# The delta rule's inverse: its transpose made on VectorE in blocks of 32 by 32, and the state's product ahead of the output's

## What is computed

```python
decay = exp(where(causal, g[:, None] - g[None, :], -inf))
m = where(strict, beta[:, None] * (k @ k.T) * decay, 0.0) + eye(C)
wu = triangular_solve(m, concatenate([k * (beta * exp(g)), v * beta]), lower=True)
w_c, u_c = wu[:, :Dh], wu[:, Dh:]
attn = (q @ k.T) * decay
def step(state, chunk):
    v_new = u_c - w_c @ state
    o = (q * exp(g)) @ state + attn @ v_new
    state = state * exp(g_last) + (k * exp(g_last - g)).T @ v_new
```

## Time and profile before

| What | Value |
|---|---|
| Time, median of 3 runs | 3366.05 us (3365.32 to 3366.66) |
| Span of the profiled execution | 3364.8 us (no time of its own is given beside it) |
| Granted TensorE clock | 0.997 of full speed |
| TensorE busy | 3322.3 us, 99% |
| VectorE busy | 2191.7 us, 65% |
| ScalarE busy | 1711.6 us, 51% |
| HBM read | 580.05 MB, 173 GB/s over the span |

### The profile page before, as it was taken

One profiled execution on the slowest core, in us unless ns is written; L12 is line 12 of the kernel. 1 busy time (PEld: TensorE's weight loads), 2 busy tenths in 40 slices (PEclk: granted clock), 3 DMA queues, 4 the chain that ended last, 5 costly groups with the idle time before them and its releaser, 6 DMA issues. The chain is left out here.

```text
span 3364.8 us, 72970 instructions
## 1 busy us (share of the span) xinstructions
PE 3322.3 (99%) x27834; PEld 3282.9 (98%) x27834; DVE 2191.7 (65%) x3584; ACT 1711.6 (51%) x2803; POOL 309.8 (9%) x314
## 2 busy tenths in 40 slices
PE   8999999999999999999999999999999999999999
PEld 7999999999999998899999999999899999999999
DVE  7667666656656666678755665665778755666655
ACT  5555644434434455656544554444665654554443
POOL 1010100000000025011002200001012101210000
PEclk9999999999999999999999999999999999999999
DMA  5234555555555554444455545555444455445554
GB/s 190 107 112 148 176 186 189 189 186 187 188 187 187 187 187 159 139 163 158 161 197 184 183 161 188 188 201 177 146 153 163 156 178 209 172 162 188 187 206 162
DMA packets 90629, 584.28 MB, mean 174 GB/s; under 512 B 10480, under 2 KB 11120, under 8 KB 28400
## 3 DMA queue, kind: packets, MB, share of 16 engines
q1 hardware_dynamic: 88992, 577.47, 48.7%
q0 software_dynamic: 1488, 4.72, 0.4%
HBM read 580.05 MB, written 2.10 MB: 173 GB/s over the span
## 5 line engine op out<-in xcount | busy, mean ns | idle before, releaser
L172 DVE TENSOR_TENSOR w_lo<-raw,w_hi 128x768 fp32r<-128x768 f32 (+5 forms) x1202 | 1378.5, 1159 | 372.6 <-ACT w_hi L161 365.6
L191 PE MATMUL bank<-h,w_hi 128*128 128x256 f32 x5168 | 1459.3, 282 | 16.5 <-DVE w_lo L172 12.0
L161 ACT ACTIVATE w_hi<-raw 128x768 fp32r<-128x768 f32 (+4 forms) x1190 | 1095.7, 968 | 692.3 <-PE bank L193 615.4
L193 PE MATMUL bank<-h,w_lo 128*128 128x256 f32 x5168 | 1444.1, 279 | 0.0
L192 PE MATMUL bank<-h,w_hi 128*128 128x256 f32 x5168 | 1443.6, 279 | 0.0
L191 PEld LDWEIGHTS bank<-h,w_hi 128*128 128x128 f32 x5168 | 973.1, 188 | 22.0 <-DVE w_lo L172 10.2
L192 PEld LDWEIGHTS bank<-h,w_hi 128*128 128x128 f32 x5168 | 973.2, 188 | 2.6 <-issue 1.9
L193 PEld LDWEIGHTS bank<-h,w_lo 128*128 128x128 f32 x5168 | 972.8, 188 | 0.0
L191 PE MATMUL bank<-mixed,w_hi 128*128 128x256 f32 x2272 | 634.9, 279 | 0.7 <-DVE w_lo L172 0.7
L193 PE MATMUL bank<-mixed,w_lo 128*128 128x256 f32 x2272 | 634.5, 279 | 0.0
L192 PE MATMUL bank<-mixed,w_hi 128*128 128x256 f32 x2272 | 633.8, 279 | 0.0
(11 more groups left out here) (408 smaller groups left out, 3340.4 us busy)
## 6 DMA issues: line engine op xcount, KB each, us to landing
raw<-in_w SPq DMA_DIRECT2D x485, 1024.0 KB, 4.8
raw<-in_w_br SPq DMA_DIRECT2D x96, 512.0 KB, 3.8
raw<-in_w_uq SPq DMA_DIRECT2D x8, 768.0 KB, 4.4
raw<-in_w_ukv SPq DMA_DIRECT2D x8, 512.0 KB, 3.3
bias_t<-in_bias POOLq DMA_DIRECT2D x16, 192.0 KB, 4.2
x<-in_x SPq DMA_DIRECT2D x4, 512.0 KB, 7.7
raw<-in_w_kr SPq DMA_DIRECT2D x4, 512.0 KB, 3.3
out_x<-x SPq DMA_DIRECT2D x3, 512.0 KB, 7.5
```

Source lines behind the costliest of these rows:

```text
L161: act.activation(w_hi[:, b % 2, c], raw[:, b, c], ACT.Copy).then_inc(S["hi_done"], 1)
L172: dve.tensor_tensor(w_lo[:, b % 2, c], raw[:, b, c], w_hi[:, b % 2, c].bitcast(F32), ALU.subtract).then_inc(S["lo_done"], 1)
L191: pe.matmul(o, w_hi[:, b % 2, c], a_hi, start=start and k == t0, stop=False)
L193: last = pe.matmul(o, w_lo[:, b % 2, c], a_hi, start=False, stop=stop and k == t0 + nt - 1)
```

## The change

- `tu` shrinks to four blocks of 128 columns. Only U is grown by products; T is made anew from U by VectorE's transpose, which turns each 32 by 32 block over in its place (`turned`), once after the first U and once after each of the first four levels. It reads and writes 128 x 256 in SBUF.
- TensorE's transposes of U (L1287 to L1289), ScalarE's copy (L570) and the products at L1305 go; the results of L1307 now lie in the first 128 columns of m[4]. The piece between the transposes and level 0 goes; levels 0 and 1 end in two pieces instead of one.
- In the chunks the product into m[5] (for the state) is issued ahead of the product into the output, and the second part of the split of unit 3 moves on VectorE from `side(8)` (ahead of the first state) to a new `side("state")` right behind it; the pool's likewise.
- After the last chunk there is one piece instead of two.

```diff
--- before.py
+++ after.py
@@ -327,8 +327,8 @@
         dec = buf("dec", SEQ)
         ddaa = buf("ddaa", [2, 2, 2, P])
         dd, aa = ddaa[:, 0, :, :, :], ddaa[:, 1, :, :, :]
-        tu_room = buf("tu", 5 * P)
-        tu = tu_room[:, 0:4 * P].rearrange("p (a k s) -> p a k s", a=2, k=2)
+        tu_flat = buf("tu", 4 * P)
+        tu = tu_flat[:, :].rearrange("p (a k s) -> p a k s", a=2, k=2)
         xm = buf("xm", [5, 2, P])
 
         def low_blocks(v, b):
@@ -339,10 +339,6 @@
 
             return v.rearrange("p (g h c) -> p g h c", h=2, c=b)[:, :, 1, :]
 
-        def grown(b):
-
-            both = tu_room[:, 0:2 * (SEQ + b)].rearrange("p (a s) -> p a s", a=2)[:, :, 0:SEQ]
-            return both.rearrange("p a (g h c) -> p a g h c", h=2, c=b)[:, :, :, 0, :]
         wu = buf("wu", [2, 2, P])
         state = buf("state", P)
         vn = buf("vn", [2, P])
@@ -566,8 +562,6 @@
                     for p in range(2):
                         act.activation(kcols[:, 2 * k + p, :], m[1][:, (src + p) * P:(src + p + 1) * P], ACT.Copy,
                                        scale=col[:, p, bass.ds(j, 1)]).then_inc(S["kcols"], 1)
-                act.wait_ge(S["t1_tr"], j + 1)
-                act.activation(tu[:, 0, :, :], m[4][:, 0:SEQ].rearrange("p (k s) -> p k s", k=2), ACT.Copy).then_inc(S["t1"], 1)
                 side(1)
                 act.wait_ge(S["wu"], j + 1)
                 act.activation(wu[:, :, :, :], m[1][:, :].rearrange("p (a k s) -> p a k s", a=2, k=2), ACT.Copy).then_inc(S["wu_sb"], 1)
@@ -829,6 +823,7 @@
                         split_lo_part(dve, i, 3, 0)
                     elif k == 8:
                         tap(i, 1, 3)
+                    elif k == "state":
                         split_lo_part(dve, i, 3, 1)
                     elif k == 9:
                         one_plus(i, 1)
@@ -886,8 +881,10 @@
                     window_sum(0)
                 elif k == 6:
                     take_pool(1)
-                elif k in (7, 8):
-                    split_lo_part(dve, B_POOL, 3, k - 7)
+                elif k == 7:
+                    split_lo_part(dve, B_POOL, 3, 0)
+                elif k == "state":
+                    split_lo_part(dve, B_POOL, 3, 1)
                 elif k == 9:
                     window_sum(1)
                 elif k == 11:
@@ -904,6 +901,10 @@
                 dve.wait_ge(S["qk_rs"], j + 1)
                 dve.scalar_tensor_tensor(q_t[:, :], pre[:, 0, :], float(P) ** -0.5, rs[:, 0, :], ALU.mult, ALU.mult).then_inc(S["q_normed"], 1)
                 dve.tensor_tensor(k_t[:, :], pre[:, 1, :], rs[:, 1, :], ALU.mult).then_inc(S["k_normed"], 1)
+
+            def turned():
+
+                dve.transpose(tu_flat[:, 0:SEQ], tu_flat[:, SEQ:2 * SEQ]).then_inc(S["t_turned"], 1)
 
             def mix(j, side, more=True):
                 dve.wait_ge(S["grow"], j + 1)
@@ -930,6 +931,8 @@
                 dve.wait_ge(S["a1"], j + 1)
                 dve.tensor_tensor(tu[:, 1, :, :], ident.unsqueeze(1).broadcast_to([P, 2, P]), tu[:, 1, :, :],
                                   ALU.subtract).then_inc(S["u1"], 1)
+                dve.wait_ge(S["u1"], j + 1)
+                turned()
                 dve.wait_ge(S["expg"], j + 1)
                 dve.tensor_tensor(qdec[:, :], q_t[:, :], expg[:, :], ALU.mult).then_inc(S["qdec"], 1)
                 side("split")
@@ -943,13 +946,12 @@
                                       level[lev].rearrange("p (g c) -> p g c", c=b), ALU.mult).then_inc(S["xm"], 1)
                     side(2 + lev)
                     dve.wait_ge(S["ltu"], k + 1)
+                    grown = high_blocks(tu_flat[:, SEQ:2 * SEQ], b)
+                    dve.tensor_tensor(grown, grown, m[4][:, 0:P].rearrange("p (g c) -> p g c", c=b),
+                                      ALU.subtract).then_inc(S["tu"], 1)
                     if lev < 4:
-                        dve.tensor_tensor(grown(b), grown(b), m[4][:, 0:SEQ].rearrange("p (a g c) -> p a g c", a=2, c=b),
-                                          ALU.subtract).then_inc(S["tu"], 1)
-                    else:
-                        last_rows = high_blocks(tu[:, 1, :, :].rearrange("p k s -> p (k s)"), b)
-                        dve.tensor_tensor(last_rows, last_rows, m[4][:, P:SEQ].rearrange("p (g c) -> p g c", c=b),
-                                          ALU.subtract).then_inc(S["tu"], 1)
+                        dve.wait_ge(S["tu"], k + 1)
+                        turned()
                 side(7)
                 dve.wait_ge(S["wu_sb"], j + 1)
                 for n in range(4):
@@ -967,6 +969,8 @@
                         else:
                             dve.scalar_tensor_tensor(state[:, :], state[:, :], expg[:, GC * n + GC - 1:GC * n + GC],
                                                      m[5][:, 0:P], ALU.mult, ALU.add).then_inc(S["state"], 1)
+                    if n == 0:
+                        side("state")
                 side(12)
                 dve.wait_ge(S["ors"], j + 1)
                 at_least(dve, "mix_hi", j)
@@ -1282,16 +1286,10 @@
                     mm = pe.matmul(m[3][:, SEQ + p * P:SEQ + (p + 1) * P], k_t[:, c], q_t[:, c], start=True, stop=True)
                 mm.then_inc(S["kkq"], 1)
                 fill(5)
-                pe.wait_ge(S["u1"], j + 1)
                 at_least(pe, "oln", j)
-                for p in range(2):
-                    mm = tr(m[4][:, p * P:(p + 1) * P], tu[:, 1, p, :])
-                mm.then_inc(S["t1_tr"], 1)
-                fill(1)
-                pe.wait_ge(S["t1"], j + 1)
                 for lev in range(5):
                     k = 5 * j + lev
-                    at_least(pe, "tu", k)
+                    pe.wait_ge(S["t_turned"], k + 1)
                     b = 2 << lev
                     for p in range(2):
                         mm = pe.matmul(m[0][:, p * GC:(p + 1) * GC].rearrange("p (g c) -> p g c", c=b), aa[:, 0, p, :],
@@ -1301,13 +1299,10 @@
                     pe.wait_ge(S["xm_zero"], 1)
                     pe.wait_ge(S["xm"], k + 1)
                     for p in range(2):
-                        if lev < 4:
-                            pe.matmul(m[4][:, p * GC:(p + 1) * GC].rearrange("p (g c) -> p g c", c=b), tu[:, 1, p, :],
-                                      low_blocks(xm[:, lev, p, :], b), start=True, stop=True)
-                        mm = pe.matmul(m[4][:, P + p * GC:P + (p + 1) * GC].rearrange("p (g c) -> p g c", c=b), xm[:, lev, p, :],
+                        mm = pe.matmul(m[4][:, p * GC:(p + 1) * GC].rearrange("p (g c) -> p g c", c=b), xm[:, lev, p, :],
                                        high_blocks(tu[:, 1, p, :], b), start=True, stop=True)
                     mm.then_inc(S["ltu"], 1)
-                    fill(1)
+                    fill(2 if lev < 2 else 1)
                 pe.wait_ge(S["tu"], 5 * j + 5)
                 pe.wait_ge(S["kcols"], 6 * j + 6)
                 for p in range(2):
@@ -1328,12 +1323,13 @@
                         pe.matmul(m[3][:, c], state[:, :], qdec[:, c], start=True, stop=False)
                         fill(1)
                     pe.wait_ge(S["vn"], 4 * j + n + 1)
+                    if n < 3:
+                        pe.matmul(m[5][:, 0:P], kcols[:, p, :], vn[:, hf, :], start=True, stop=True).then_inc(S["ds"], 1)
                     mm = pe.matmul(m[3][:, c], vn[:, hf, :], aa[:, 1, p, GC * hf:GC * hf + GC], start=n == 0, stop=True)
                     if n < 3:
-                        pe.matmul(m[5][:, 0:P], kcols[:, p, :], vn[:, hf, :], start=True, stop=True).then_inc(S["ds"], 1)
                         fill(1)
                 mm.then_inc(S["o_done"], 1)
-                fill(2)
+                fill(1)
                 pe.wait_ge(S["osq"], j + 1)
                 pe.matmul(m[4][:, 0:SEQ], ones, osq[:, :], start=True, stop=True).then_inc(S["oss"], 1)
                 fill(2)
```

## The result

The changed kernel takes 3371.65 us (median of 20 runs, 3367.28 to 3377.82) against 3366.19 us for the kernel before (20 runs, 3364.71 to 3368.11): 5.5 us more, ratio 1.0017 with a 95% interval of 1.0011 to 1.0023. The forecast was 3369.0 us, 2.9 more. The profiled execution took 3371.84 us, its span is 3370.2 us.

A forecast was written before the change was run, and what follows sets the result against it. TensorE, 99% busy, bounds the kernel; per head 2.08 us of work and some 1.6 us of idle stand against about 4 us of new idle and restarts. Sum: 5 x 0.37 + 1.08 = 2.9 us, 3369.0 us; range 3360 to 3379.

The forecast's parts named there:

- What bounds, and where: TensorE, 99% busy, bounds the six heads; removed passes count in full unless it stops for VectorE's queue.
- the replay: TensorE's and VectorE's timelines through one head, rerun in the new order: a regular head becomes 0.37 us longer.
- The transpose's price: Each of five 128x256 block transposes per head on VectorE takes 0.42 us, as elementwise operations of that size do.
- The bounds of 0.28 and 0.79: Ends for the block transpose's time: 0.28 us from a half-wide plain copy, 0.79 us from L928.
- rival 2: A slow transpose of 0.79 us lies on the path: 1.56 us per head, 9.4 us, time 3378.4; chance 0.25.
- The waits: TensorE idles 0.59 us at the front, 1.03 at level 0, 1.11 and 0.23 ahead of levels 3 and 4, 0.67 at second state.
- The state's part: In the chunks: the first state's 0.62 us wait goes, the second's grows; 0.44 us behind becomes 0.33.
- The last head: Pool's work in VectorE's queue holds level 4's block and the second state: 1.08 us longer.
- The sum: Five regular heads of 0.37 us more plus 1.08 for the last: 2.9 us more, 3369.0 us.
- Rival 1: Work counts, waits don't: without the two long stalls, 12.8 us over six heads, time 3356.2; chance 0.12.
- Rival 3: Units 1 to 3 needed up to a piece earlier: 0 to 0.3 us per head, 3370.8; no separate chance, within forecast's range.

The follow-up runs named there:

- level 0's order: Changed kernel with, at level 0 alone, xm ahead of VectorE's 1.48 us split and the tap behind the transpose: 3364.2 us beside 3367.4 for the kernel before.
- the split behind the transpose: Changed kernel with level 2's 1.48 us weight split behind the block transpose instead of ahead of the subtraction: 3369.8 us beside 3365.9 for the kernel before.
- the gates: Changed kernel with the four gate columns (last head: pool's second window) behind the second state instead of ahead: 3370.6 us beside 3365.9 for the kernel before.
- the doubled transpose: Changed kernel with each block transpose made twice, the first into an unused buffer: 3381.6 us, ratio 1.0047 to the kernel before.
- the transposes alone: Changed kernel with the output's product first again and unit 3's split back ahead of the first state: 3380.2 us, ratio 1.0038 to the kernel before.
- the full version: Changed kernel with level 0's xm early, taps behind transposes, large splits and pieces rearranged, gates behind second state: 3358.2 us beside 3365.9; again 3359.8 beside 3367.8.
- the order alone: Kernel before, no block transposes, state's product first, unit 3's second split and gates later, level 2's large split behind the subtraction: 3365.0 us beside 3367.8.
- the kernels with both waits: Five kernels: the changed one, transposes alone, each transpose twice, level 2's split moved, gates moved; times 3371.65, 3380.2, 3381.6, 3369.8 and 3370.6 us.
- the state's part without the transposes: Kernel before with only the state's product issued first and unit 3's second split behind the first state: 3367.2 us beside 3367.4, ratio 1.0002.

## Why the prediction was right, and what it missed

- **What bounds, and where.** Right. TensorE lost 18 passes per head and got longer heads; the waits stand where the replay put them. Shifted by 79.99 us, the starts that the replay gave for a level's first product (L1297, now L1295), levels 0 to 4, and for the stage behind them were 101.70, 105.92, 108.94, 112.37, 115.00, 117.40; the trace has 101.76, 106.03, 109.04, 112.46, 115.13, 117.53. The products with the first state (120.32, less 0.18, and one more piece of 0.70) and the second were forecast for 120.84 and 124.04 and came at 120.97 and 124.13.
- **The transpose's price.** 0.445 us, against 0.42 taken from the elementwise rows. The estimate from the Trainium skill (VectorE: DVE Perf Modes, The three transpose paths) was 0.44 and is the one that the trace bears out. The bounds of 0.28 and 0.79 weren't needed; rival 2, the slow transpose, falls. That L928 takes 0.79 us because its two inputs disturb each other was a guess that no run tests.
- **The waits.** Forecast 0.59, 1.03, 1.11, 0.23 and 0.67 us, counted in pitches. The profile counts idle from the end of the last matmul, and shows 0.48, 0.92, 0.97 and 0.40 for the first, second, third and last. Counted in pitches the rows above give 0.64, 1.07, 1.13, 0.26 and 0.56, the fourth from 194.86 to 195.12, too short for the profile's list. Confirmed one by one: by level 0's order, by the split behind the transpose, by the gates, and by the doubled transpose, whose 1.5 us per head came out as replayed.
- **The state's part.** Right in kind (one wait gone, the next grown), 0.17 us gained per head instead of 0.11 (0.44 behind to 0.33), without the transposes (38.77 to 38.60) and with them (38.34 to 38.17).
- **The last head.** 1.01 us more (35.90 to 36.91 between its first matmul and the output's norm), forecast 1.08.
- **The sum.** 2.9 us forecast, 5.5 measured. The term that is missing is the clock; the prediction put it at nothing without a word. The prediction took every matmul's pitch from rows at full clock and didn't ask what two waits of together 1.4 us within 3 us do to it. In the changed kernel the granted clock falls after them in some heads and costs 1.6 us each time; one fall in the profiled execution accounts for 1.6 of the 4.83 us that its heads grew, and the rest, 3.2, is the forecast's 2.9 and a few hundredths per head, the transpose's 0.03 among them. In the kernel with the transposes alone it was the larger part: five falls, 8 of 12.8 us. So it took some luck that the time stayed near the forecast: the same two waits, with as many falls as there, would have taken it past the 6.7 us that the prediction counts as none. The upper end of its range, 3379, was set for a slow transpose, not for this.
- **Rival 1** (the work counts, the waits don't) is wrong for the change as it was made; without the waits it would have been right in part: with the queue laid out anew the kernel is 7.7 us faster than before (8.0 in the second set), not 22.
- **Rival 3** (the splits' due times): no sign of it in the changed kernel: the waits for a split in this stretch are one of 0.8 us in the first head, 0.6 before, and the one of 0.6 us behind the heads, as before. It is real where the pool's window was moved: 2.0 us there.

## What to carry to other kernels

Where one engine is near 100% busy, work taken from it counts only as far as the engine that takes it over can deliver in time at that place in its queue; an average of 69% busy says nothing of that, and a replay of both queues with rows of the trace gives it to a tenth of a microsecond. When a step moves to an in-order engine, look at what is queued just ahead of the step and of the next one: here moving one weight split of 1.48 us behind a masking of 0.29 us was worth 1.0 us per head, and by the times of the runs, the clock's falls among them, more (5.5 us above the kernel before to 3.2 below it) than the 5.2 us that the full version has over the order alone. Follow each such move to the end of the stretch: moving the pool's window took away a wait of 0.8 us and made another one 1.3 us longer. And count short waits of TensorE that follow each other closely as a risk for its clock, not only as their own length.

## What the runs showed of the hardware

- The granted clock of TensorE can fall after two waits that together are well under 2 us, 0.5 and 0.9 us, with TensorE busy for 1.68 of the 3 us around them. It then stays at the lower level for about 3.4 us (0.60 on average over 4 us, 0.97 over the next 4) and costs 1.6 us here. It doesn't always fall: it did in 11 of the 30 heads of the kernels with both waits, in one of six in the changed kernel and in five of six with the transposes alone, and in none of the profiled execution with the longest waits (heads of 40.7 us). With the second wait gone it fell in none of 42 heads; the times of two pairs of kernels, each in another session than its partner, agree (3371.65 to 3364.2 us, 3380.2 to 3363.6). What decides between the heads with both waits was not settled.
- A block transpose of 128x256 float32 takes 0.445 us within SBUF, 0.02 more than the subtraction of the same size ahead of it (L932, 0.425 us on average), and the next independent operation starts 0.37 us after it.
- A group of four passes that starts after a wait lasts 0.66 us, one that follows without a gap 0.55 or 0.56 (L1295 at 192.45 and at 186.02): even a short wait has a restart of 0.1 us behind it.
- The clock falls elsewhere too: between 360 and 380 us, behind the heads, the granted clock is 0.91 in the kernel before and in the changed one alike, and half of the twelve profiled executions show such a fall between 350 and 380 us; eleven show one between 16 and 30 us. The execution that has neither (the state's part without the transposes, 3365.10 us) is the fastest of its kernel's eleven. How much of the spread between runs is of that kind was not measured.
